# Attention of a hybrid block: value products of two query blocks in one group, 16 groups for 48, in another order of blocks

## The reference, cut to what matters

```python
for start in range(0, S, SB_BLOCK):                     # query blocks of 128
    z = einsum('bhqd,bhkd->bhqk', qb, kb) * scale       # keys 0 .. end of the block
    valid = k_pos[None, :] < q_pos[:, None]
    log_keep = where(valid, log_sigmoid(-z), 0.0)
    later = cumsum(log_keep, axis=3, reverse=True) - log_keep
    w = where(valid, exp(log_sigmoid(z) + later), 0.0)
    outs.append(einsum('bhqk,bhkd->bhqd', w, vb))
```

## Time and profile before

| | us |
|---|---|
| median of 3 runs | 985.21 |
| lowest and highest | 984.68, 985.76 |
| span of the profiled execution | 982.9 |
| PE busy | 944.2 (96%) |
| DVE, ACT, POOL busy | 534.3, 326.0, 212.4 |

### The profile page before, as it was taken

The page is one execution under the profiler, slowest core; times in us unless marked ns, Lnnn a source line. Parts: engine busy times, 40 slices in busy tenths (PEclk is TensorE's granted clock), DMA queues, the critical chain, the costliest instruction groups (busy, mean ns, idle before and its releaser), DMA issues.

```text
span 982.9 us, 13739 instructions
## 1 busy us (share of the span) xinstructions
PE 944.2 (96%) x5507; PEld 784.6 (80%) x5507; DVE 534.3 (54%) x770; ACT 326.0 (33%) x732; POOL 212.4 (22%) x122
## 2 busy tenths in 40 slices
PE   3799999999999999999999999999999989999998
PEld 3688889877777788888877888888888768787886
DVE  4876999688867354454043265123335457655322
ACT  7642222577776321212621110222223542110000
POOL 0003423520001022111322111100010026773000
PEclk9999999999999999999999999999999999999999
DMA  9851603510220211210313435412112774435321
GB/s 320 244 174 30 183 5 108 153 39 16 57 52 11 76 43 49 59 43 25 98 51 106 130 95 160 100 43 65 54 44 84 258 257 129 150 111 211 101 92 65
DMA packets 122665, 100.55 MB, mean 102 GB/s; under 512 B 18055, under 2 KB 104672, under 8 KB 122346
## 3 DMA queue, kind: packets, MB, share of 16 engines
q1 hardware_dynamic: 92298, 76.07, 25.6%
q10 hardware_dynamic: 30304, 23.60, 7.9%
HBM read 73.44 MB, written 24.12 MB: 99 GB/s over the span
## 4 chain that ended last, share of the span: by engine, by line
PE 77%; DVE 7%; DMA 5%; ACT 4%; POOL 3%; issue 3%; SPq 1%; ACTq 0%; DVEq 0%
PE psum L819 37%; PE psum L266 5%; PE psum L267 5%; PE psum L268 5%; PE psum L654 5%; PE psum L1065 3%; DMA sg<-z_scratch 3%; PE psum L1050 2%; PE psum L656 2%; DVE stick L1167 2%; PE psum L1036 2%; PE psum L1400 1%; ACT sg L1974 1%; POOL hlo L2003 1%; PE psum L1038 1%
## 5 line engine op out<-in xcount | busy, mean ns | idle before, releaser
L819 PE MATMUL psum<-hhi,w3hl 128*128 128x512 f32 x1120 | 368.9, 399 | 4.2 <-issue 3.5
L819 PEld LDWEIGHTS psum<-hhi,w3hl 128*128 128x128 f32 x1120 | 210.3, 188 | 50.2 <-issue 7.6
L819 PE MATMUL psum<-hlo,w3hl 128*128 128x512 f32 x560 | 218.3, 390 | 0.0
L808 POOL TENSOR_TENSOR w3hl<-w3raw,w3hl 128x1024 fp32r<-128x1024 f32 x43 | 104.6, 2432 | 492.9 <-DVE w3hl L801 492.9
L819 PEld LDWEIGHTS psum<-hlo,w3hl 128*128 128x128 f32 x560 | 105.4, 188 | 21.3 <-issue 1.9
L1167 DVE TENSOR_TENSOR_SCAN stick<-stick,floor 128x1024 f32<-128x1024 f32 (+7 forms) x64 | 90.7, 1456 | 21.0 <-ACT stick L1113 20.8
L819 PE MATMUL psum<-ohi,w3hl 128*128 128x512 f32 x256 | 79.3, 390 | 2.8 <-issue 2.8
L801 DVE CAST w3hl<-w3raw 128x1024 fp32r<-128x1024 f32 x43 | 34.0, 790 | 72.8 <-DMA w3raw<-in_w_in 32.5
L903 ACT COPY zst<-psum 128x512 f32<-128x512 f32 x44 | 25.9, 589 | 130.4 <-PE psum L819 124.5
L654 PE MATMUL psum<-w,hhi 128*128 128x512 f32 x192 | 67.5, 396 | 0.0
L819 PEld LDWEIGHTS psum<-ohi,w3hl 128*128 128x128 f32 x256 | 48.0, 188 | 13.5 <-issue 3.6
(11 more groups left out here) (226 smaller groups left out, 1581.0 us busy)
## 6 DMA issues: line engine op xcount, KB each, us to landing
z_scratch<-zst ACTq DMA_DIRECT2D x44, 256.0 KB, 2.1
w3raw<-in_w_in ACTq DMA_DIRECT2D x20, 512.0 KB, 4.2
ada<-in_ada_w SPq DMA_DIRECT2D x16, 512.0 KB, 6.4
w3raw<-in_w_in SPq DMA_DIRECT2D x16, 512.0 KB, 4.1
sg<-z_scratch SPq DMA_DIRECT2D x8, 1024.0 KB, 5.0
xrow<-in_x SPq DMA_DIRECT2D x4, 1024.0 KB, 6.1
w1raw<-in_w_in SPq DMA_DIRECT2D x4, 1024.0 KB, 7.1
adag<-in_ada_w SPq DMA_DIRECT2D x8, 512.0 KB, 4.6
```

The costliest lines, as they stand in the source:

```text
L808: nc.gpsimd.tensor_tensor(lo, w3raw[:], cast(hi), ALU.subtract).then_inc(w3_lo, 1)
L819: t = nc.tensor.matmul(out_, a[:, kt, :], moving[b][:, kt, 512 * half:512 * half + 512], start=(ends[0] and kt == k0 and m == 0), stop=(en ...
```

## The change

The blocks of a pair are taken in the order 7, 0, 1, 6, 5, 2, 3, 4. Two neighbours then have nine key blocks together and their four steps (a quad) fill the six slots exactly. `values(quad)` multiplies all of it at once: it waits for the sixth copy of the quad (`w_ok`), and all copies of the next quad wait for it (`v_mm`). It stands at step 4q + 5, between the scores and the flips of PE's step. The two output blocks lie side by side in bank 7 and are copied out one after the other at step 4q + 6, and stored in twos. Since block 4 now ends a pair and its scores need banks 1 and 3, they wait for the turns' `low` (`fl_ok`).

```diff
-        steps = [(pair, qb, head) for pair in range(PAIRS) for qb in range(ST - 1, -1, -1) for head in range(2)]
+        ORDER = (7, 0, 1, 6, 5, 2, 3, 4)
+        steps = [(pair, qb, head) for pair in range(PAIRS) for qb in ORDER for head in range(2)]
...
-        def o_bank(m):
-            return bank(7)
+        def o_cols(m):
+            return bank(7)[:, P * (m % 2):P * (m % 2) + P]
...
+                if n % PER in (PER - 2, PER - 1) and pair + 1 < PAIRS:
+                    pe.wait_ge(fl_ok, 4 * (pair + 1) + 3 + n % 2)
...
-            def values(m, a):
-                pair, qb, _ = steps[2 * m]
-                pe.wait_ge(w_ok, tile_of[2 * m + 1, a] + 1)
-                if a == 0:
+            def values(quad):
+                pe.wait_ge(w_ok, NW * (quad + 1))
+                if quad == 0:
+                    pe.wait_ge(ve_ok, 1)
+                else:
+                    pe.wait_ge(o_ok, 2 * quad)
+                for m in range(2 * quad, 2 * quad + 2):
+                    pair, qb, _ = steps[2 * m]
                     pe.wait_ge(dv_ok, pair + 1)
...
-            for n in range(NST + 5):
+            for n in range(NST + 2):
...
+                if n >= 5 and n % 4 == 1:
+                    values((n - 5) // 4)
                 if 1 <= n <= NST:
                     flips(n - 1)
-                m, a = (n - 3) // 2, (n - 3) % 2
-                if n >= 3 and (m, a) in part_of:
-                    values(m, a)
...
                 if t >= NW:
-                    act.wait_ge(v_mm, reader[t - NW] + 1)
+                    act.wait_ge(v_mm, t // NW)
...
-            for n in range(NST + 6):
-                m = (n - 4) // 2
-                if n >= 5 and n % 2 and m < NST // 2 and steps[2 * m][1] >= 4:
-                    copy_out(m)
-                if n >= 4 and n % 2 == 0 and m < NST // 2 and steps[2 * m][1] < 4:
-                    copy_out(m)
+            for n in range(NST + 3):
+                if n >= 6 and n % 4 == 2:
+                    for m in range((n - 6) // 2, (n - 6) // 2 + 2):
+                        copy_out(m)
```

More of the change, by code:

```diff
@@ L930, in chunks @@
             return range(steps[n][1] // 4 + 1)
-        tile_of, first_tile, part_of, last_part = {}, [], {}, []
+        tile_of, first_tile = {}, []
         for n in range(NST):
@@ L936, in hybrid_block @@
                 tile_of[n, a] = len(tile_of)
[L937 to L940, removed]
         first_tile.append(len(tile_of))
-        reader = {}
-        for (n, a), t in tile_of.items():
-            reader[t] = part_of[n // 2, a]
+        assert all(first_tile[n] == NW * (n // 4) for n in range(0, NST, 4))
         TURNS = ((1, 0), (1, 1), (0, 1), (0, 0))
@@ L992, in sp_2 @@
             load_w3(sp, 1)
-            for n in range(NST + 5):
+            for n in range(NST + 4):
                 if n == 2 * PER:
@@ L998, in sp_2 @@
                     second_half(u)
-                m = (n - 5) // 2
-                if n >= 5 and n % 2:
-                    pair, qb, _ = steps[2 * m]
-                    sp.wait_ge(o_ok, m + 1)
-                    sp.dma_start(o_dram[pair, :, P * qb:P * qb + P], ost[:, m % 2]).then_inc(o_out[m % 2], 16)
+                if n >= 7 and n % 4 == 3:
+                    for m in range((n - 7) // 2, (n - 7) // 2 + 2):
+                        pair, qb, _ = steps[2 * m]
+                        sp.wait_ge(o_ok, m + 1)
+                        sp.dma_start(o_dram[pair, :, P * qb:P * qb + P], ost[:, m % 2]).then_inc(o_out[m % 2], 16)
             for b in range(2):
@@ L1052, in flips @@
                     f.then_inc(t_mm, 1)
-            def values(m, a):
-                pair, qb, _ = steps[2 * m]
-                pe.wait_ge(w_ok, tile_of[2 * m + 1, a] + 1)
-                if a == 0:
-                    pe.wait_ge(dv_ok, pair + 1)
[L1059 to L1068, removed]
+            def values(quad):
[5 more added lines that the diff above has]
+                for m in range(2 * quad, 2 * quad + 2):
+                    pair, qb, _ = steps[2 * m]
+                    pe.wait_ge(dv_ok, pair + 1)
+                    for kb_ in range(qb + 1):
+                        for head in range(2):
+                            h0 = HD * head
+                            v = nc.tensor.matmul(o_cols(m)[h0:h0 + HD],
+                                                 rows[:, 2, kb_, P * pair + h0:P * pair + h0 + HD],
+                                                 wT_slots[tile_of[2 * m + head, kb_ // 4] % NW][:, kb_ % 4],
+                                                 start=kb_ == 0, stop=kb_ == qb, skip_group_check=True)
                 v.then_inc(v_mm, 1)
@@ L1124, in copy_out @@
                 pair, qb, _ = steps[2 * m]
-                act.wait_ge(v_mm, last_part[m])
+                act.wait_ge(v_mm, m // 2 + 1)
                 if m == 0:
@@ L1129, in copy_out @@
                     act.wait_ge(o_out[m % 2], 16 * (m // 2))
-                nc.scalar.activation(ost[:, m % 2], o_bank(m)[:, 0:P], ACT.Identity,
+                nc.scalar.activation(ost[:, m % 2], o_cols(m), ACT.Identity,
                                      bias=vTe[:, pair, qb:qb + 1]).then_inc(o_ok, 1)
```

## The result

The changed kernel takes **992.7 us** (median of 4 runs, 991.2 to 994.7) where the kernel before takes 984.9 on the same chip (4 runs, 984.4 to 985.8): a ratio of 1.0074, with an interval of 1.0059 to 1.0089. It is slower by 7.3 us by the ratio and by 7.8 between the medians; the two profiled executions lie 6.5 apart. Forecast were 7.1. All comparisons are between fast executions, and one of the four of experiment 4's twin, which took 4498 us, is left out of them.

A forecast was written before the change was run, and what follows sets the result against it. The prediction took PE to bound the attention stage: 10.6 us saved on value groups against 17.7 us of added waits gave +7.1 us on 985.2, a forecast of 992.3 us, range 988 to 996.

The forecast's parts named there:

- PE bounds the stage: In the attention stage of 135.55 us PE is busy 130.4 us, DVE 101.5 and ACT 99.8, so PE bounds it.
- A group costs 0.33 us: Each group of value products costs PE 0.33 us beside its products; 32 fewer groups save 10.6 us.
- Kind 1: Value blocks on PE wait for ACT's last copy of their quad: eleven of sixteen wait, 7.1 us.
- Kind 2: Block 4's scores wait for DVE's `low` of turns 2 and 3 in banks 1 and 3: three pairs, 6.0 us.
- Kind 3: PE's flips, with two banks, wait for ACT's copies: 23 flip groups wait 0.1 to 1.4 us, 11.1 us.
- The sum of waits: PE's attention waits come to 24.4 us, where the walk of the order before has 6.7: +17.7 us.
- A block takes 2.25 us: Four steps' value products on PE form one block of 18 matmuls, 2.25 us, sixteen times.
- ACT 97% loaded outside the blocks: ACT does one sigmoid per block, so 87 us must fit into 89; sign: ACT waits some 20 us for L1063.
- Small edits: Paired stores, smaller scans and the last output copies cost nothing; nothing else in the span moves by over 0.5 us.
- Waits covered: Rival: group saving real, attention waits after below 17.3 us in total; -7.6 us, 977.6 us, chance 0.13.
- they cancel: Rival: attention waits of 15 to 19 us offset the group saving; 985 us, chance 0.15.
- The forecast's own test: The forecast fails if PE's idle time in the attention stage stays under 15 us.

The follow-up runs named there:

- experiment 4: Changed kernel, block 4's last 128 keys left out of scores and sigmoid in the first three pairs, wait for banks 1 and 3 removed: 987.75 us, ratio 1.0026.
- experiment 4's twin: Changed kernel, the same 128 keys of block 4 left out in the first three pairs, but the wait for DVE's subtractions kept: ratio 1.0096.
- 8: Kernel before, old order, one value group per query block but blocks 1 and 0 together, 28 groups for 48: 978.5 us, ratio 0.9938.
- 10: Kernel before, old order, one value group per query block but blocks 1 and 0, and 3 and 2, together, 24 groups: 978.1 us, ratio 0.9926.
- experiments 6 and 7: Kernel before plus 32 identity transposes, either ahead of value groups (989.8 us) or in their middle, cutting each in two (998.7 us).
- experiment 5: Changed kernel with seven slots for six and the value block behind the flips of its step: 991.5 us, ratio 1.0056.
- Experiment 1: Kernel before with the new block order and its wait for banks 1 and 3, still 48 value groups: 985.0 us, ratio 1.0007.
- experiment 9: Changed kernel with the last pair's blocks in the order 3, 4, 5, 2, 7, 0, 6, 1: 992.3 us, ratio 1.0069.

## Why the prediction was right, point by point

- **PE bounds the stage, 135.55 us.** Holds: what took PE's time away (8, 10) shortened it by the same amount, and ACT and DVE were nowhere busy for more than 105 us of it.
- **A group costs 0.33 us, 32 of them 10.6.** Holds in mechanism, a little high in size: 0.27 to 0.30 by experiments 6 and 7, 8.6 to 9.6 in all.
- **Kind 1, blocks wait for their last copy, 7.1 us in 11 places.** Right in place and number, high in size: 10 waits of PE, 4.9 us (7.6 counted from its weight loads).
- **Kind 2, block 4's scores wait for DVE, 6.0 us.** Right in mechanism: 6 waits, 4.2 us (5.6). Taking it away saved 5.7 us in the medians and 6.75 in the stage (4), of which only 2.0 are idle time of PE; most of the rest fits two clock drops less.
- **Kind 3, flips wait for copies, 11.1 us in 23 places.** The term that was mis-sized most: 10 waits for ACT, 6.8 us. My walk let every small lateness of ACT reach PE; more than half of those places were covered.
- **The sum of waits, +17.7.** Measured +13.5 to +14.5. One term was left out: the forecast took all work at the full clock, because the stage before ran at 1.00 throughout. Behind the new waits the clock fell, which cost 2.9 us in the profiled execution. So the total of +7.1 was met in part by luck: waits too long by 3 to 4 us and groups too dear by about 1, against no clock, nearly cancel.
- **A block takes 2.25 us.** It takes 2.12 from its first product on, and 0.09 ahead of it: 2.21. Sixteen blocks are 0.6 us shorter than in the forecast.
- **ACT 97% loaded outside the blocks.** Its busy time is 96.3 us, and experiment 5, which relieved it in the block, took the waits of kind 1 away and gave no gain clear of the noise. The load was a fair warning of waits, but "a block stops ACT" was the smaller part of the mechanism. The sign given for it, ACT waiting some 20 us for L1063, didn't show as such: the profile puts 3.7 us to L1063 and 32.3 to the flips behind the blocks.
- **Small edits at nothing, rest of the span unchanged within 0.5.** The rest is 0.9 us shorter, more than the 0.5, in one profile of each. Experiment 1 shows the order at 0.1 us; it has the old stores, so the stores in twos were not run by themselves.
- **The rivals.** "Waits covered" put its border at 17.3 us in total after; counted as there (the walk's 6.7 of before and 13.5 to 14.5 more) they came to 20 or 21, too many for it, and too many for "they cancel" with its 15 to 19. The forecast's own test, PE idle over 15 us in the stage, came out at 16.7, narrowly.

## What to carry to other kernels

To merge small groups of another matmul shape saves 0.3 us for each group, but those groups are also what PE does while the helpers finish a step: merge neighbours only while every step keeps some of them. Ask of each saving on the bounding engine what it was covering; the same merging down to 28 groups gave 0.7%, down to 16 it cost 0.7%.

## What the runs showed of the hardware beyond that

Short waits of PE can cost more than their length. Behind waits of 1.3 to 1.8 us, some with shorter ones beside them, the granted clock fell from 1.00 to 0.50, the value products ran at 0.21 us instead of 0.109, and each of the two drops in the kernel after cost 1.4 or 1.5 us. The Trainium skill (TensorE: Matmul & The Clock Gate, HAM oscillation — how this bites in real kernels) describes such an alternation for a kernel whose PE waits for DMA; here waits for ACT and DVE of under 2 us came ahead of it.

It doesn't happen each time: the same passage with the same waits kept the full clock in the kernel after and lost it in experiment 9, and the end of the stage, with other last steps, lost it in the kernel after and kept it in 9. The kernel before has one wait of 1.4 us for DVE in the stage and kept 1.00 throughout. What decides it these runs don't tell. Whether such waits also widen a kernel's spread they don't show: the four runs of the kernel after lie 3.5 us apart and those of the kernel before beside them 1.4, but 21 runs of the latter on another chip lie 5.5 apart.
